# Summing squares of centred conformer channels with a one-column matmul, token sums on partitions, in place of a ones-matrix product and its diagonal

## The reference, cut to what matters

```python
def _layernorm(x, g, b):
    mu = jnp.mean(xf, axis=-1, keepdims=True)
    var = jnp.mean(jnp.square(xf - mu), axis=-1, keepdims=True)
    y = (xf - mu) * lax.rsqrt(var + EPS)
    return (y * g + b)
...
c = _causal_depthwise_conv(u, w_conv_dw) + b_conv_dw     # 1024 tokens x 512 channels
y_conv = jax.nn.silu(_layernorm(c, ln_conv_g, ln_conv_b))
```

## Time and profile before

| | |
|---|---|
| median of 3 runs | 1361.3 us (1359.85 to 1364.41) |
| the profiled execution | 1361.3 us, span in the profile 1359.5 us |
| PE, DVE, ACT, POOL busy | 1149.3, 621.2, 320.8, 242.0 us |
| mean granted TensorE clock | 0.932 of full speed |
| GDN stage | from about 320 to 528 us of the span |

### The profile page before, as it was taken

How to read it: one execution, slowest core, us unless ns; L and a number is a source line. 1 busy time by engine, 2 the same in 40 slices (tenths; PEclk the granted TensorE clock), 3 DMA queues, 4 the chain that set the end, 5 groups by cost and what they waited for, 6 DMA issues and landing times. The chain is left out here.

```text
span 1359.5 us, 16853 instructions
## 1 busy us (share of the span) xinstructions
PE 1149.3 (85%) x6294; PEld 747.8 (55%) x6294; DVE 621.2 (46%) x904; ACT 320.8 (24%) x691; POOL 242.0 (18%) x347
## 2 busy tenths in 40 slices
PE   6999899997778886999989888888897878872997
PEld 5888788875667775887533333333332223321885
DVE  5799999974667755332621111111111111124573
ACT  5212111125544535221321000000111000022332
POOL 4000100012674541000121111111111111100120
PEclk9999999998889987999889888888999898885999
DMA  6111111200000103321799999999799999975431
GB/s 205 32 47 32 47 47 47 62 0 1 1 2 1 64 2 116 141 78 47 317 397 422 423 423 423 419 417 403 285 420 423 424 424 417 416 306 205 151 126 62
DMA packets 70243, 281.22 MB, mean 207 GB/s; under 512 B 12649, under 2 KB 38442, under 8 KB 53546
## 3 DMA queue, kind: packets, MB, share of 16 engines
q1 hardware_dynamic: 57120, 258.53, 48.0%
q0 software_dynamic: 9456, 16.80, 3.2%
q10 hardware_dynamic: 3610, 5.11, 1.0%
HBM read 268.34 MB, written 29.62 MB: 219 GB/s over the span
## 5 line engine op out<-in xcount | busy, mean ns | idle before, releaser
L2308 PE MATMUL ps_u<-wup,xgT 128*64 128x512 f32 x1024 | 261.3, 669 | 61.8 <-DMA wup<-in_w_up_dram 59.4
L2308 PEld LDWEIGHTS ps_u<-wup,xgT 128*64 128x64 f32 x1024 | 87.5, 153 | 234.3 <-issue 233.1
L94 PE MATMUL ps_b<-n_hi,wh 128*128 128x512 f32 x384 | 157.7, 411 | 0.7 <-DVE wl L418 0.7
L2235 DVE TENSOR_TENSOR hb<-sil,ps_u 128x256 f32<-128x256 f32 x32 | 13.5, 421 | 305.0 <-ACT sil L2182 305.0
L94 PE MATMUL ps_b<-n_lo,wh 128*128 128x512 f32 x384 | 151.9, 396 | 0.0
L94 PE MATMUL ps_b<-n_hi,wl 128*128 128x512 f32 x384 | 151.9, 396 | 0.0
L94 PEld LDWEIGHTS ps_b<-n_hi,wh 128*128 128x128 f32 x384 | 73.2, 191 | 16.5 <-issue 2.5
L94 PEld LDWEIGHTS ps_b<-n_hi,wl 128*128 128x128 f32 x384 | 73.0, 190 | 16.3
L94 PEld LDWEIGHTS ps_b<-n_lo,wh 128*128 128x128 f32 x384 | 73.3, 191 | 15.1 <-issue 1.0
L2182 ACT ACTIVATE sil<-ps_u 128x256 f32<-128x256 f32 x32 | 12.3, 384 | 292.7 <-PE ps_u L2308 292.7
L461 DVE SCALAR_TENSOR_TENSOR convT<-upad,vecT,convT 128x1024 f32<-128x1024 f32 (+1 forms) x75 | 79.9, 1066 | 0.0
(11 more groups left out here) (361 smaller groups left out, 1919.4 us busy)
## 6 DMA issues: line engine op xcount, KB each, us to landing
wup<-in_w_up_dram SPq DMA_DIRECT2D x64, 2048.0 KB, 17.7
zT<-in_w_down_dram SPq DMA_DIRECT2D x32, 1024.0 KB
convT<-in_w_down_dram SPq DMA_DIRECT2D x32, 1024.0 KB, 18.7
wraw<-in_w_in_dram SPq DMA_DIRECT2D x24, 512.0 KB, 4.2
convT<-y_rows SPq DMA_DIRECT2D x16, 512.0 KB, 4.5
qkvT<-in_x_dram SPq DMA_DIRECT2D x8, 512.0 KB, 8.6
qkvT<-in_w_out_dram SPq DMA_DIRECT2D x8, 512.0 KB, 5.3
xr<-in_x_dram SPq DMA_DIRECT2D x8, 512.0 KB, 3.8
```

Of the source, the lines that this page charges most:

```text
L94: ins = nc.tensor.matmul(ps, lhs[a], rhs[b], start=first and k == 0, stop=last and k == 2)
L2235: nc.vector.tensor_tensor(hb[k][rows], sil[k][rows], ps_u[k][rows, FE:2 * FE], ALU.mult).then_inc(s_h, 1)
L2308: last = nc.tensor.matmul(ps_u[k][HC[c], :], xgT[k][:, j, HC[c]], wup[k][c][:, j, :], start=j == 0, stop=j == NJ - 1)
```

## The change

TensorE's `channel_squares` takes the squares as the stationary operand and one column of `ones` as the moving one: for each of 2 token tiles, 4 products of a 128 x 128 tile of `sqn` with a 128 x 1 column, summed in one column of `n_sq2`. The token then is on the partition as it comes out. The multiplication by the identity, the reduction and their two waits leave VectorE; one instruction (L1140 in the old numbering) reads the two columns, scales by 1/512 and adds EPS. The scale leaves ScalarE's squaring. All eight products stand in one place, between `change(i, 1)` and `read_out(i, 1)`. The next pair's `level_u(3, 1)` waits for `ms` in place of `dg`.

```diff
--- before.py
+++ after.py
@@ -749,7 +749,7 @@
 
         n_sq, n_rs = sem("norm_sq"), sem("norm_rs")
         p_nrm = Steps(sem("pe_nrm"), ["sum0", "var0"] + [f"{n}{i - k}" for i in range(1, NP2) for n, k in (("sum", 0), ("row", 1), ("var", 0))] + [f"row{NP2 - 1}"])
-        v_nrm = Steps(sem("dve_nrm"), ["dev0", "dg0", "sv0", "ms0"] + [f"{n}{i - k}" for i in range(1, NP2) for n, k in (("nrm", 1), ("dev", 0), ("dg", 0), ("sv", 0), ("ms", 0))] + [f"nrm{NP2 - 1}"])
+        v_nrm = Steps(sem("dve_nrm"), ["dev0", "ms0"] + [f"{n}{i - k}" for i in range(1, NP2) for n, k in (("nrm", 1), ("dev", 0), ("ms", 0))] + [f"nrm{NP2 - 1}"])
 
         with ExitStack() as c4:
             def two(name, shape=F4):
@@ -773,7 +773,7 @@
             vt, rt_ = rs[:, 0:2], ss[:, 0:2]
             A = [[psum(f"ps_ga{g}{n}", F4, ctx=c4) for n in G2] for g in G2]
             lent = [A[1][n][:].rearrange("p h c -> p (h c)") for n in G2]
-            n_mean, n_var = lent[0][:, 0:2 * P], lent[1][:, 0:2 * P]
+            n_mean, n_sq2 = lent[0][:, 0:2 * P], lent[1][:, 0:2]
             n_rows = [lent[i == NP2 - 1][:, 2 * P:4 * P] for i in range(NP2)]
             Bk = [psum(f"ps_gb{n}", F4, ctx=c4) for n in range(4)]
             LR = A[0][1][:].rearrange("p h c -> p (h c)").rearrange("p (n j m) -> p n j m", n=2 * H, j=BS)
@@ -865,7 +865,7 @@
                     act.wait_ge(*v_nrm.sem_at(f"dev{i}"))
                     if i:
                         act.wait_ge(*p_nrm.sem_at(f"row{i - 1}"))
-                    nc.scalar.activation(sqn[:], convT[:, :, columns(i)], ACT.Square, scale=float(CF) ** -0.5).then_inc(n_sq, 1)
+                    nc.scalar.activation(sqn[:], convT[:, :, columns(i)], ACT.Square).then_inc(n_sq, 1)
 
                 def channels_out(i):
                     act.wait_ge(*v_nrm.sem_at(f"nrm{i}"))
@@ -1131,13 +1131,7 @@
 
                 def mean_squares(i):
                     dve.wait_ge(*p_nrm.sem_at(f"var{i}"))
-                    wide = [P, 2, P]
-                    nc.vector.tensor_tensor(RD, n_var.rearrange("p (g c) -> p g c", g=2), ident[:].unsqueeze(1).to_broadcast(wide),
-                                            ALU.mult).then_inc(*v_nrm(f"dg{i}"))
-                    dve.wait_ge(*v_nrm.sem_at(f"dg{i}"))
-                    nc.vector.tensor_reduce(vt, RD, axis=AX.X, op=ALU.add).then_inc(*v_nrm(f"sv{i}"))
-                    dve.wait_ge(*v_nrm.sem_at(f"sv{i}"))
-                    nc.vector.tensor_scalar(vt, vt, EPS, None, ALU.add).then_inc(*v_nrm(f"ms{i}"))
+                    nc.vector.tensor_scalar(vt, n_sq2, 1.0 / CF, EPS, ALU.mult, ALU.add).then_inc(*v_nrm(f"ms{i}"))
 
                 def norm_columns(i):
                     dve.wait_ge(*p_nrm.sem_at(f"row{i}"))
@@ -1287,7 +1281,7 @@
                         if i:
                             pe.wait_ge(*a_two.sem_at(f"Y6{g}", i - 1))
                             if g:
-                                pe.wait_ge(*v_nrm.sem_at(f"dg{i - 1}"))
+                                pe.wait_ge(*v_nrm.sem_at(f"ms{i - 1}"))
                     else:
                         pe.wait_ge(*(g_one.sem_at(f"m4{g}", i) if l == 4 else g_two.sem_at(f"m5{g}", i)))
                         pe.wait_ge(*v_two.sem_at(f"X{l - 1}{g}", i))
@@ -1365,12 +1359,12 @@
                         last = mm(n_mean, ones[:], convT[:, m, columns(i)], m == 0, m == NC_ - 1)
                     last.then_inc(*p_nrm(f"sum{i}"))
 
-                def channel_squares(i, parts):
+                def channel_squares(i):
                     pe.wait_ge(n_sq, i + 1)
-                    for m in parts:
-                        last = mm(n_var, ones[:], sqn[:, m, :], m == 0, m == NC_ - 1)
-                    if m == NC_ - 1:
-                        last.then_inc(*p_nrm(f"var{i}"))
+                    for g in G2:
+                        for m in range(NC_):
+                            last = mm(n_sq2[:, g:g + 1], sqn[:, m, g * P:(g + 1) * P], ones[:, 0:1], m == 0, m == NC_ - 1)
+                    last.then_inc(*p_nrm(f"var{i}"))
 
                 def channel_rows(i):
                     pe.wait_ge(n_rs, 2 * i + 2)
@@ -1440,9 +1434,8 @@
                     read_out(i, 0)
                     read_state(i, 1)
                     solve(i, 1)
-                    channel_squares(i, range(NC_ // 2))
                     change(i, 1)
-                    channel_squares(i, range(NC_ // 2, NC_))
+                    channel_squares(i)
                     read_out(i, 1)
                     if ahead:
                         blocks(i + 1)
```

## The result

The changed kernel takes 1371.9 us (median of 20 runs, 1364.5 to 1380.4) against 1362.6 us for the kernel before (20 runs). The ratio is 1.0077, with an interval of 1.0059 to 1.0094: slower by 0.6 to 0.9%, some 8 to 13 us. The forecast was 1364.9 and the range ended at 1368.5. The profiled execution has a span of 1375.3 us and a time of 1377.1, so it is one of the slower runs of the changed kernel; sums over its trace come out larger than the median difference.

What follows compares the result with a forecast made beforehand. It took the GDN stage's chain of waits from the read-out as the bound. Four pairs at +0.91 us, VectorE at 0, gave 1361.3 + 3.6 = 1364.9 us, range 1360.0 to 1368.5.

Steps and rivals of the forecast that it cites:

- The chain from the read-out: In the GDN stage, a microsecond between dS1 and the read-out delays all four engines and costs the kernel four times.
- VectorE's part at nothing: The 844 ns a pair removed from VectorE only lengthen its wait for GpSimd's root; taken as 0.
- The price of a one-column instruction: On TensorE, the 128 x 128 load sets the pace of the squares: 0.111 us each, 1.78 us for 16.
- the cheap-load rival: Loads under one column are cheap, at 0.032 us the squares gain 1.4 us: 1359.9; chance 0.13.
- The sum by pace and place: Squares behind dS1 take 1.78 us where 0.87 stood: +0.91 us a pair, +3.6 us over four pairs.
- the clock's term: Slow stretches at each pair's start may gain or lose two groups, 0.9 us each: 1363 to 1367.
- Its own sign of being wrong: The prediction would be wrong if, among other signs, TensorE's slow stretches moved by more than two groups.
- The clock falls earlier: Longer idle time before dS1, then one-column work, slows TensorE: 1367.5 at chance 0.13, or 1382 at 0.03.
- The argument that held the rival down: Against an earlier clock fall: the stretch before is at full clock through waits of 1.00 us.
- The forecast's 1.2 us of idle time before dS1: TensorE was to idle some 1.2 us before dS1, in place of 0.32, once the first half moved away.

Runs made afterwards that it cites:

- the filled kernel: The changed kernel with two unread old products (four matmul instructions of 256 columns) added in the wait before dS1; 1365.1 us, ratio 1.0016.
- the split kernel: The changed kernel with tile 0's one-column products in the wait before dS1 and tile 1's behind dS1; 1365.3 us, ratio 1.0007.
- the fastest kernel here: The kernel before, its squares' second half behind tile 0's output turn in pairs 0 to 2, VectorE's three steps behind both scalings; 1356.3 us, ratio 0.9952.

## Why the prediction was wrong, point by point

- **The chain from the read-out** was read rightly: 0.85 us more between dS1 and the read-out came out at 0.93 us more between AR1 and tile 1's scaling in pair 0, with no wait that took it up.
- **VectorE's part at nothing** was right: with the two steps put back neither the time nor the distances in the trace changed.
- **The price of a one-column instruction** was right: 0.111 us, two of them to a product. The load of 128 x 128 sets the pace, as the nearest rows said, and the cheap-load rival with its 0.032 us is out. The passage of the Trainium skill with 25 ns for small products ("TensorE: Matmul & The Clock Gate", section "Back-to-back issue gap") gives the gap of the matmul alone and says itself that this leaves the loads out; it does not fit here, where each instruction brings a new float32 stationary operand and the starts are 111 ns apart. Its section "LDWEIGHTS (loading the stationary operand)", by whose formula a load of 128 columns takes 107 ns, agrees.
- **The sum by pace and place**, +3.6 us, was right for the path: in the profiles of the filled kernel and of that with 32 columns, where no slow stretch falls on the squares, AR1 to tile 1's scaling is 0.92 to 0.93 us longer in each of the four pairs, 3.7 in all. The whole time of the filled kernel is, by the ratio, +2.2 (0.3 to 4.2). The +3.7 of the kernel with 128 columns is near the sum by luck, for it has slow stretches in it.
- **The clock is the step that failed.** "I allow two either way: 1363 to 1367" sized the clock's term from the next pair's first level alone, and took both signs for equally likely. Its own sign of being wrong, slow stretches that move by more than two groups, came true. The rival "The clock falls earlier" named the mechanism, one column at a time behind a longer idle time, with 0.13 at one group a pair (1367.5) and 0.03 at everything slow (1382). What happened lies between them: 9.4 us in all by the medians and 8 to 13 by the ratio's interval, which leaves some 4 to 9 us of clock on top of the 3.6, in a kernel whose runs spread from 1364.5 to 1380.4 with it. The argument that held the rival down, full clock through waits of 1.00 us, was about the kernel before, in which the stretch from AR1 on has 256-column work in it. The forecast's 1.2 us of idle time before dS1 was too much as well: the changed kernel's rows have 0.78 before its matmuls, less than the 1.00 and 1.13 before AR1, and still the clock falls there. The length of one wait does not foretell the fall.
- The full loss takes both. With the wait filled the one-column products ran at full clock, at a ratio of 1.0016; the split kernel is at 1.0007, with a spread that leaves some clock loss possible. Without the low column count (128 columns, or the old products moved) the clock fell at dS1 but came back sooner, and the ratios were 1.0027 and 1.0033. With both they were 1.0052 (VectorE's steps put back), 1.0060 (32 columns) and 1.0077. Within one group of runs the step is seen as well: 128 columns against one (VectorE's steps put back) 1367.4 and 1371.5 us, the wait filled against 32 columns with the wait left 1365.1 and 1371.8.

Open is how the loss grows between 32 and 128 columns, which was not tried, and why single executions of the changed kernel differ by 16 us: a profile shows one of them. Over 53 of its executions the correlation of time and mean clock is -0.83, so that the clock goes with most of it; where in each the clock fell, and why it held in pair 0 of the profiled one, is not shown.

## What to carry to other kernels

A matmul inside a wait of TensorE can be more than free: here 256-column work in a wait kept the clock up for what followed, while one-column work did so before dS1 in the profiled executions and not in the wait for tile 1's root. Before work is moved out of a wait or made narrower, look at where the stretches at half clock lie and at what stands on the path behind the wait. A matmul instruction with few columns costs its load, here 0.11 us for 128 x 128 float32 whether 1, 8, 32 or 128 columns follow, and a float32 product is two of them. One profile of a kernel whose time varies with the clock shows one execution only: look at the spread of its runs and their mean clocks too. Work that nobody awaits goes into the waits of the chain and, in the other engine's queue, behind the instruction that the chain waits for: so the fastest kernel here was made.

## What the runs showed of the hardware that was not expected

- Four useless matmul instructions of 256 columns, put where the changed kernel's dS1 waits for 0.78 us, made it 7 us faster (1371.9 to 1365.1, ratios 1.0077 and 1.0016), 0.87 us of added work in each of four pairs against the clock of everything behind it.
- In the wait for tile 1's root, four 256-column instructions (busy for 1.03 us) went with a next level of 1.15 us in five of six pairs of two kernels, and eight or sixteen one-column instructions (busy for 0.95 or 1.84 us) with 1.97 or 1.98 us in five of six. TensorE's busy time in the profile does not tell the two apart; the granted clock does. These kernels differ in the width of the squares before dS1 too, so that the wait alone is not shown to make the difference.
- A kernel can have the same median as another and a much wider spread: the split kernel has 1365.3 us and runs from 1359.0 to 1373.7, the filled one 1365.1 and 1362.3 to 1369.6.
